# Every RMS norm of a two-layer hybrid decoder in two token halves, with the units around it

## The reference

```python
def _rmsnorm(x, g):
    xf = x.astype(jnp.float32)
    y = xf * lax.rsqrt(jnp.mean(xf * xf, axis=-1, keepdims=True) + EPS)
    return (y * g.astype(jnp.float32)).astype(x.dtype)

def _modulate(h, shift, scale):
    return h * (1.0 + scale[:, None, :]) + shift[:, None, :]

def reference(x, c, norm_mix_g, w_in, w_ret_out, w_sb_out, w_mix_out, norm_mlp_g,
              w_up, w_down, w_ada, b_ada, final_g):
    c_act = jax.nn.silu(c)
    for l in range(DEPTH):
        mod = c_act @ w_ada[l] + b_ada[l]
        shift1, scale1, gate1, shift2, scale2, gate2 = jnp.split(mod, N_MOD, axis=-1)
        h = _modulate(_rmsnorm(x, norm_mix_g[l]), shift1, scale1)
        x = x + gate1[:, None, :] * _mixer(h, w_in[l], w_ret_out[l], w_sb_out[l], w_mix_out[l])
        h2 = _modulate(_rmsnorm(x, norm_mlp_g[l]), shift2, scale2)
        u = jnp.square(jax.nn.relu(h2 @ w_up[l]))
        x = x + gate2[:, None, :] * (u @ w_down[l])
    return _rmsnorm(x, final_g)
```

## Time and profile before

| | us |
|---|---|
| median of three runs (lowest, highest) | 2421.44 (2421.01, 2422.19) |
| the profiled execution | 2421.1 |
| its span in the trace | 2419.4 |
| TensorE busy in the span | 2372.0 |
| VectorE, ScalarE, GpSimd busy | 1012.5, 904.9, 1125.2 |

### The profile page before, as it was taken

How to read it: one execution, slowest core, us unless ns; L and a number is a source line. 1 busy time by engine, 2 the same in 40 slices (tenths; PEclk the granted TensorE clock), 3 DMA queues, 4 the chain that set the end, 5 groups by cost and what they waited for, 6 DMA issues and landing times.

```text
span 2419.4 us, 29753 instructions
## 1 busy us (share of the span) xinstructions
PE 2372.0 (98%) x11994; PEld 1985.2 (82%) x11994; DVE 1012.5 (42%) x1513; ACT 904.9 (37%) x1037; POOL 1125.2 (47%) x1486
## 2 busy tenths in 40 slices
PE   6999999999999999999999999999999999999998
PEld 5888888888887878888878888888888787888886
DVE  6676566624442341221356666440444423221223
ACT  3223233256667332332333222233556843332332
POOL 2444544543434545554644454444434345554552
PEclk7999999999999999999999999999999999999999
DMA  7443535322212323323243544223122123223231
GB/s 236 161 156 120 166 123 163 122 70 70 66 57 70 105 79 95 105 87 105 87 140 124 173 132 134 92 70 105 54 69 70 53 88 95 96 87 105 92 100 53
DMA packets 244152, 252.46 MB, mean 104 GB/s; under 512 B 4016, under 2 KB 241728, under 8 KB 244032
## 3 DMA queue, kind: packets, MB, share of 16 engines
q1 hardware_dynamic: 242496, 247.53, 31.8%
q10 hardware_dynamic: 1536, 3.17, 0.4%
HBM read 248.59 MB, written 2.10 MB: 104 GB/s over the span
## 4 chain that ended last, share of the span: by engine, by line
PE 96%; DVE 1%; ACT 1%; DMA 1%; issue 0%; SPq 0%; DVEq 0%; ACTq 0%
PE proj L701 65%; PE proj L738 11%; PE proj L723 7%; PE att L843 4%; PE att L795 2%; PE att L828 1%; PE att L777 1%; PE att L855 1%; PE proj L668 1%; PE att L687 1%; DVE slab L966 1%; PE att L804 1%; DMA work<-in_w_ada 0%; DMA ya<-in_x 0%; PE att L660 0%
## 5 line engine op out<-in xcount | busy, mean ns | idle before, releaser
L366 POOL TENSOR_TENSOR w_lo<-w_raw,w_hi 128x256 fp32r<-128x256 f32 x1472 | 1123.0, 794 | 1257.6 <-ACT w_hi L405 1256.6
L405 ACT ACTIVATE w_hi<-w_raw 128x1024 fp32r<-128x1024 f32 x368 | 385.1, 1054 | 560.5 <-PE proj L701 473.6
L701 PE MATMUL proj<-h_hi,w_hi 128*128 128x512 f32 x1504 | 591.3, 393 | 0.0
L701 PE MATMUL proj<-h_lo,w_hi 128*128 128x512 f32 x1504 | 587.3, 390 | 0.0
L701 PE MATMUL proj<-h_hi,w_lo 128*128 128x512 f32 x1504 | 586.8, 390 | 0.0
L701 PEld LDWEIGHTS proj<-h_hi,w_lo 128*128 128x128 f32 x1504 | 283.2, 188 | 59.8
L701 PEld LDWEIGHTS proj<-h_hi,w_hi 128*128 128x128 f32 x1504 | 283.1, 188 | 58.9 <-issue 0.3
L701 PEld LDWEIGHTS proj<-h_lo,w_hi 128*128 128x128 f32 x1504 | 283.3, 188 | 57.3
L701 PE MATMUL proj<-y_lo,w_hi 128*128 128x512 f32 x832 | 323.8, 389 | 0.0
L701 PE MATMUL proj<-y_hi,w_lo 128*128 128x512 f32 x832 | 323.8, 389 | 0.0
L701 PE MATMUL proj<-y_hi,w_hi 128*128 128x512 f32 x832 | 323.8, 389 | 0.0
(11 more groups left out here) (153 smaller groups left out, 2522.3 us busy)
## 6 DMA issues: line engine op xcount, KB each, us to landing
w_raw<-in_w_in SPq DMA_DIRECT2D x88, 1024.0 KB, 5.1
slab<-in_w_ada SPq DMA_DIRECT2D x40, 1024.0 KB, 7.7
w_raw<-in_w_up SPq DMA_DIRECT2D x32, 1024.0 KB, 5.5
w_raw<-in_w_down SPq DMA_DIRECT2D x32, 1024.0 KB, 5.0
w_raw<-in_w_ret_out SPq DMA_DIRECT2D x16, 1024.0 KB, 5.0
work<-in_w_ada SPq DMA_DIRECT2D x8, 1024.0 KB, 5.5
w_raw<-in_w_sb_out SPq DMA_DIRECT2D x8, 1024.0 KB, 5.0
w_raw<-in_w_mix_out SPq DMA_DIRECT2D x8, 1024.0 KB, 5.0
```

The source lines that it names most:

```text
L366: ins = pool.tensor_tensor(w_lo[:, s, ks, :], w_raw[:, s // 2, ks, P * (s % 2):P * (s % 2 + 1)], w_hi[:, s, ks, :], ALU.subtract)
L405: act.activation(w_hi[:, 2 * s + j, :, :], w_raw[:, s, :, P * j:P * (j + 1)], ACT.Copy).then_inc(hi_ready, 1)
L701: last = pe.matmul(proj[:, j, :], w[:, slot, k, :], a[:, k, :], start=k == 0 and n == 0, stop=k == KT - 1 and n == 2)
```

## The change

All five norms go in two halves of 256 tokens (`HALVES`). `normed_unit` takes the place of `first_unit` behind a norm and `tail_unit` that of the two half units ahead of it; both run all tiles of the first token half before the second, with matmuls of 256 columns. In `tail_unit` the first token half of the products goes to `proj`, the second to banks 4 and 5 of `att`. The mean square of the first half stands in the middle of the second half's products, that of the second half stands inside `normed_unit`. ScalarE and VectorE run the adds, squares, roots, scalings and splits per half, the second half's add and square placed between the first half's tiles. ScalarE splits the weights of the second unit behind a norm in four pieces between steps 6 and 9. The first up unit of the later quarters runs as `whole_unit`. The final scalings go by half too, and the transposes are taken in the order `OUT_ORDER`. The load of the rotary table for layer 1 moves to the end of the norm ahead of layer 0's MLP; eight memsets of `ya` in the last quarter of the last layer go; `y_T` moves to another place in `work`.

```diff
+OUT_ORDER = [(t + 2 * pair, half) for pair in range(2) for half in range(2) for t in range(2)]
-BY_TILE = (1, 1, 1, 1, 1, 3)
+HALF = SEQ // 2
+HALVES = (slice(0, HALF), slice(HALF, SEQ))
+NORM_STEPS = 2 * KT
...
             for t in range(TB):
-                sp.wait_ge(y_stored, t + 1)
-                sp.wait_ge(y_stored_dve, t + 1)
+                sp.wait_ge(y_stored_dve if t % 2 == 0 else y_stored, 2 * (t // 2 + 1))
...
+            def tail_first(n, pair, unit, buffers):
+                for j in range(2):
+                    added(pair, unit, j)
+                    square_half(n, 6 + j, 0, buffers)
+                root(n, 0)
+                act.wait_ge(tail_added, 2 * n - 1)
+                square_half(n, 6, 1, buffers)
...
+            def norm_tail(n, pair, unit, buffers):
+                tail_first(n, pair, unit, buffers)
+                for g in range(NORM_STEPS):
+                    high_half(n, g)
+                    if g == 3:
+                        tail_second(n, buffers)
+                    if g == 4:
+                        root(n, 1)
+                    if g in (6, 8):
+                        products(pair, unit, (g - 6) // 2)
+                    if 6 <= g < 10:
+                        split_weights(pair, unit + 2, (g - 6) // 2, g % 2)
...
+            def tail_unit(n, pair, unit, hi, lo, buffers):
+                for t in range(2):
+                    for j in range(2):
+                        slot = 2 * (unit % 2) + j
+                        if t == 0:
+                            pe.wait_ge(lo_ready, 4 * pair + 2 * unit + j + 1 + LO_CREDIT)
+                            pe.wait_ge(bank_free[j], 2 * pair + unit + 1)
+                        dst = proj[:, j, HALVES[0]] if t == 0 else tail_late(j)
+                        for k in range(KT):
+                            if (t, j, k) == (1, 0, KT // 2):
+                                mean_square(n, 0, buffers)
+                            for m, (w, a) in enumerate(((w_hi, hi), (w_hi, lo), (w_lo, hi))):
+                                last = pe.matmul(dst, w[:, slot, k, :], a[:, k, HALVES[t]],
+                                                 start=k == 0 and m == 0, stop=k == KT - 1 and m == 2)
+                        last.then_inc(tail_done if t == 0 else proj_done, 1)
+            def normed_unit(n, pair, unit, buffers):
+                for t in range(2):
+                    k0 = 0
+                    for step in (1, 1, 1, 1, 1, 1, 1, 1) if t == 0 else (1, 1, 1, 1, 4):
+                        for j in range(2):
...
+                            for k in range(k0, k0 + step):
+                                if j == 0:
+                                    pe.wait_ge(h_ready, NORM_STEPS * n + KT * t + k + 1)
...
+                        if n > 0 and t == 0 and k0 == 2:
+                            mean_square(n, 1, buffers)
...
-                        if m == 0:
-                            first_unit(pair, MLP, h_hi, h_lo, normed_ready(2 * layer + 1), BY_TILE)
...
+                        if m == f == 0:
+                            normed_unit(2 * layer + 1, pair, MLP, at_mlp)
+                        else:
+                            whole_unit(pair, MLP + m, h_hi, h_lo)
...
+            def scale_step(n, g):
+                k, t = g % KT, g // KT
+                if k == 0:
+                    dve.wait_ge(rstd_ready, 2 * n + t + 1)
+                if g >= 2:
+                    dve.wait_ge(h_ready, NORM_STEPS * n + g - 1)
+                dve.scalar_tensor_tensor(scaled(g), x_T[:, k, HALVES[t]], n_scale[:, ds(KT * n + k, 1)],
+                                         rstd_of(t), ALU.mult, ALU.mult).then_inc(x_normed, 1)
...
+                between = {0: lambda: add_tail(n, 0, 1, pair, unit, gate_col),
+                           2: lambda: add_last_square(n, 1, buffers),
+                           3: lambda: add_tail(n, 1, 1, pair, unit, gate_col)}
...
+            for n, (t, half) in enumerate(OUT_ORDER):
+                if n % 2 == 0:
+                    dve.wait_ge(y_turned, n + 1)
+                    dve.tensor_copy(x_tok[:, t, SEQ * half:SEQ * (half + 1)], turned_out(t, half)).then_inc(y_stored_dve, 1)
```

More of the change, by code:

```diff
@@ L408, in products, with added @@
             def products(pair, unit, j):
                 act.wait_ge(proj_done, 4 * pair + 2 * unit + j + 1)
[L412 to L416, removed]
-                act.activation(rstd, rstd, ACT.Exp, scale=-0.5).then_inc(rstd_ready, 1)
[L419 to L430, removed]
+            def added(pair, unit, half):
+                act.wait_ge(bank_free[half], 2 * pair + unit + 2)
@@ L619, in down @@
                 def down(pair, last):
-                    for m in range(4):
+                    for m in range(3 if last else 4):
                         for half in range(2):
                             products(pair, MLP + 4 + m, half)
-                            if not last or m < 2 or (layer < DEPTH - 1 and (m, half) != (3, 1)):
+                            if not last or m < 2 or layer < DEPTH - 1:
                                 split_weights(pair, MLP + 4 + m + 2, half)
@@ L627, in down @@
                                 square(2 * layer + 2, 2 * m + half, at_layer)
+                    if last and layer < DEPTH - 1:
+                        norm_tail(2 * layer + 2, pair, MLP + 7, at_layer)
+                    elif last:
+                        tail_first(2 * DEPTH, pair, MLP + 7, at_layer)
+                        tail_second(2 * DEPTH, at_layer)
+                        root(2 * DEPTH, 1)
                 for f in range(QUARTERS - 1):
@@ L633, in _ @@
                 down(first + 4 * (QUARTERS - 1), True)
[L636 to L639, removed]
+            for n, (t, half) in enumerate(OUT_ORDER):
+                if n % 2 == 1:
+                    act.wait_ge(y_turned, n + 1)
+                    act.activation(x_tok[:, t, SEQ * half:SEQ * (half + 1)], turned_out(t, half), ACT.Copy).then_inc(y_stored, 1)
         @block.tensor
@@ L755, in _ @@
             for layer in range(DEPTH):
                 first = layer * LAYER_PAIRS
-                mean_square(2 * layer, at_layer)
+                if layer == 0:
+                    for t in range(2):
+                        mean_square(0, t, at_layer)
                 for i in range(RET_LOOPS):
@@ L1046, in add_to_x, with add_tail @@
                                               x_T[:, k, :], ALU.mult, ALU.add), half)
+            def add_tail(n, j, t, pair, unit, gate_col):
+                gate, x = mod[:, ds(gate_col + 6 + j, 1)], x_T[:, 6 + j, HALVES[t]]
+                if t == 0:
+                    dve.wait_ge(tail_done, 2 * n - 1 + j)
+                    free(dve.scalar_tensor_tensor(x, proj[:, j, HALVES[0]], gate, x, ALU.mult, ALU.add), j)
+                else:
+                    products(pair, unit, j)
+                    dve.scalar_tensor_tensor(x, tail_late(j), gate, x, ALU.mult, ALU.add).then_inc(tail_added, 1)
@@ L1052, in _ @@
                     scale_and_shift(0, 0)
-                norm(2 * layer, at_layer)
+                    norm(0, {})
                 for i in range(RET_LOOPS):
@@ L1220, in _ @@
                 gates = MODS * KT * layer
-                for m in range(8):
+                for m in range(7):
                     for half in range(2):
@@ L1235, in _ @@
                             add_to_x(first, SB_OUT + m, half, k, gates + KT * GATE1)
-                norm(2 * layer + 1, at_mlp)
+                norm_tail(2 * layer + 1, first, MIX + 3, gates + KT * GATE1, at_mlp)
                 def quarter(pair, f, last):
@@ L1242, in quarter @@
                             n = KT * (4 * layer + f) + k
-                            if last:
+                            if last and layer < DEPTH - 1:
                                 dve.memset(ya[:, k, :], 0.0)
@@ L1256, in quarter @@
                             add_to_x(pair, MLP + 4 + m, half, k, gates + KT * GATE2)
+                    if last:
+                        norm_tail(2 * layer + 2, pair, MLP + 7, gates + KT * GATE2, at_layer, layer == DEPTH - 1)
                 for f in range(QUARTERS - 1):
```

190 lines of the change are left out of this document (121 added, 69 removed).

## The result

The changed kernel takes 2408.91 us (median of six runs, 2406.86 to 2411.37), the kernel before beside it 2421.34 (six runs, 2421.01 to 2422.47): a ratio of 0.9948 with a 95% interval of 0.9935 to 0.9961. Forecast were 2409.0 and a gain of 12.4 us; 12.4 came. The profiled execution took 2407.28, its span is 2405.6, that is 13.8 less than the span of before.

What follows compares the result with a forecast made beforehand. TensorE, 96% of the chain of waits, bounds the kernel, with holes at norms and MLP quarter starts; -9.1 + 0.85 + 0.4 - 3.0 - 1.5 = -12.4 from 2421.1 gives 2408.7, stated as 2409; range 2402 to 2418.

Steps and rivals of the forecast that it cites:

- Prices of halved work: VectorE's scaling over 256 columns taken at 0.48 us, one tile's step from scale to scale at 0.91 instead of 1.45.
- Rival A: VectorE's halved operation costs only 0.41 us, saving 7 us more in four norms: 2402; chance 0.10.
- rival C: VectorE's norm steps take 0.62 us beside GpSimd's remainders, so the kernel gets slower: 2427; chance 0.07.
- The inner norms: Three norms inside the program: the 6.5 us hole and the clock's fall go, gains 3.41, 3.12 and 2.59: -9.1 us.
- rival D: Last square misses TensorE's slot or ScalarE is held; each inner norm loses 2 to 4 us: 2415 to 2421; chance 0.09.
- Rival B: TensorE's clock falls all the same in the second token half; inner norms lose 6.95 us again: 2416; chance 0.16.
- the argument against B from the quarters: After waits of 0.4 us at the MLP quarters, matmuls run on at 0.2267 us.
- The norm at the start and the banks: Halves hide nothing at the first norm, +0.85 us; VectorE frees the first bank some 0.2 late, +0.4 us.
- The quarters: MLP quarters after the first no longer wait for the last add at their start: six times 0.50, -3.0 us.
- The end: Final norm and output: first block issued at 20.6 instead of 21.44, fourth landing at 27.2 instead of 28.7: -1.5 us.
- the second root "at 16.05": Final norm: VectorE gets the second half's root 16.05 us after the last unit's start, mean square behind eight transposes ending 15.1.
- The limit by the transfers: Four output blocks of 512 KB take 1.3 us each, holding the end's gain to -1.5 us instead of -3.8.

Runs made afterwards that it cites:

- Run b: The changed kernel with four instead of two buffers for the scaled half tiles: 2402.47 us, ratio 0.9923.
- Run c: The changed kernel with the first norm, n = 0, whole again over 512 tokens, all others in halves: 2408.72 us.
- run e: The kernel before with only the MLP quarters after the first running their first unit half by half, norms whole: 2418.56 us, ratio 0.9988.
- run d: The changed kernel with VectorE's first two output copies placed between the final scalings instead of behind the sixteenth: 2406.81 us.
- run a: The changed kernel timed and profiled again with no edit: 2409.46 us.
- f: The changed kernel with the third batch of conditioning products (sixteen one-column matmuls) moved behind the next half unit: 2402.55 us, ratio 0.9921.
- i: The version of f with TensorE's wait for VectorE's last sum put back at the old place, the small matmuls still moved: 2405.44 us.

## Why the prediction was right, point by point

- *Prices of halved work.* 0.48 was taken for VectorE's operation; 0.479 to 0.489 is the mean over all four norms (below), and 0.475 that of the sixteen final scalings. The step of 0.91 is exact. Rival A (0.41) and rival C (0.62) needed other durations, and none of these groups shows them. Run b shows that the step is what the norm hangs on: taking 0.12 off it took 1.2 us off each inner norm.

```profile
L1150 DVE SCALAR_TENSOR_TENSOR att<-x_T,n_scale,att 128x256 f32<-128x256 f32 x64 | 31.2, 489 | 11.8 <-ACT att L446 9.5
L1157 DVE SCALAR_TENSOR_TENSOR h_lo<-att,n_shift,h_hi 128x256 fp32r<-128x256 f32 x64 | 30.6, 479 | 3.1 <-ACT h_hi L454 3.1
```

- *The inner norms.* The last square met TensorE's slot (7.19 against 7.20, and the matmul that takes it, L809, follows at 866.20 without a break), so rival D did not occur. The last tile was to reach TensorE at 25.78; its matmuls begin at 884.17, which is 25.76 behind the first matmul of the unit ahead (858.41 in TensorE's timeline). The end of the unit was forecast at 27.58 and read at 27.65. The gain of 9.1 came as 8.8.
- *Rival B.* The working of TensorE at six matmuls in every 0.91 did not cost the clock: 1.00 in the stretch where the earlier trace rows has 0.59. The trace thus bears out the argument against B from the quarters, and not the analogy to the swinging clock that the Trainium skill reports ("TensorE: Matmul & The Clock Gate", section "A second HAM failure mode: psum-queue depth-cycling"). Where the clock did swing was a place that the change doesn't touch.
- *The norm at the start and the banks.* +0.85 and +0.4 forecast, +1.0 and +0.57 read. Run c, which undoes both at n = 0, gave 0.8 back; its whole norm is 0.46 slower than that of before, which stays unexplained.
- *The quarters.* -3.0 forecast; -3.09 in the changed kernel's chain; alone, in run e, -3.1 in the chain and -2.9 in the time.
- *The end.* This term was mis-sized: -1.5 forecast, -2.71 read. The step that failed is the second root "at 16.05". It came at 2394.13 - 2379.13 = 15.0, because the eight transposes ahead of its mean square took 0.88 (two rows of 0.44 for four). The prediction gives them no price, but from the end of the unit ahead (12.37) to that of the mean square (15.1, 0.85 of it its own) it leaves 1.88. All behind it moved with it: the first issue to 19.5 from 20.6. The limit by the transfers was right, and run d shows it: an earlier first block was worth 2.0 us.
- *Where the total came from.* The terms of the change were forecast at -12.4 and read at -13.05: the end gave 1.2 more, and the start, the banks and the inner norms together 0.6 less. The two medians differ by 12.4 all the same, and that exact agreement is chance: the profiled execution of the changed kernel has one fall of the clock at the three places, before's has two and run a's three. More falls are a likely part of the upper group of times, but this isn't shown, since none of that group was profiled.

## What to carry to other kernels

Halving a norm pays where another unit's matmuls fill the time between root and first tile: the hole and the fall of the clock behind it went together (no run takes them apart), while a norm with nothing ahead of it only became longer. Once the hole is closed, the time is the slowest engine's step by the number of tiles, so look next for a wait inside that step (here for a buffer, 0.12 of 0.91, worth 1.2 us a norm). Where the times of a kernel fall into groups, compare the granted clock place by place in two executions before explaining a stage's difference by the edit.

## What was not expected of the hardware

- A wait of 0.68 us with sixteen matmuls of one column right behind it was followed by a lower granted clock (0.90 over 17 us, against 1.00) in some executions and not in others, worth 1.6 us each time; either of the two alone left it at 1.00 in the profiled execution and the times within 0.75 us of each other (f, i).
- A wait of TensorE cost more than the view of waits says: 0.95 us a place at full clock where the view has 0.68 (i).
- Sixteen matmuls of one column took 1.70 us from the first one's start to the start of the next wide one in the midst of other work (1437.69 to 1439.39, f), and 1.81 right behind a wait (1436.87 to 1438.68, the changed kernel).
